# Cumulative sums of the gates as split single-pass products in a two-layer hybrid backbone

## The reference

```python
def gla_chunked(q, k, v, logg, s0, with_output=True):
    g = jnp.cumsum(logg.astype(f32).reshape(b, n, GLA_CHUNK, h, dk), axis=2)     # chunks of 64 positions
    g_last = g[:, :, -1]
    k_upd = k * jnp.exp(g_last[:, :, None] - g)
    ds = jnp.einsum('bnjhd,bnjhv->nbhdv', k_upd, v)
    decay = jnp.moveaxis(jnp.exp(g_last), 1, 0)
    ...                                           # scan of the states over the chunks
    g_mid = g[:, :, GLA_CHUNK // 2 - 1][:, :, None]
    scores = jnp.einsum('bnihd,bnjhd->bnhij', q * jnp.exp(g - g_mid), k * jnp.exp(g_mid - g))
    scores = jnp.where(mask, scores, 0.0)
    o_intra = jnp.einsum('bnhij,bnjhv->bnihv', scores, v)
    o_inter = jnp.einsum('bnihd,nbhdv->bnihv', q * jnp.exp(g), s_start)
    return (o_intra + o_inter).reshape(b, l, h, dv), s_final
...
logg_f = jax.nn.log_sigmoid((lr_f @ w_dec_f + b_dec_f).astype(jnp.float32)) / GLA_TAU
...
o = o_f + flip(o_b)                               # both directions, 4 heads, dk = 64, dv = 128
o = o * lax.rsqrt(jnp.mean(o * o, axis=-1, keepdims=True) + RMS_EPS)
y_gla = (o * gla_norm_w).reshape(b, l, GLA_V_W) * jax.nn.silu(r)
y = jnp.concatenate([y_gla, y_four, y_conv], axis=-1) @ w_out
```

## Time and profile before

| | us |
|---|---|
| median of three runs | 1609.99 |
| the profiled execution, its own time | 1608.07 |
| its span, first to last instruction | 1606.3 |
| TensorE busy in the span | 1542.8 (96%) |
| DVE, ScalarE, GpSimd busy | 861.7, 568.2, 592.9 |
| mean granted TensorE clock | 0.988 |

### The profile page before, as it was taken

The page is one execution under the profiler, slowest core; times in us unless marked ns, Lnnn a source line. Parts: engine busy times, 40 slices in busy tenths (PEclk is TensorE's granted clock), DMA queues, the critical chain, the costliest instruction groups (busy, mean ns, idle before and its releaser), DMA issues.

```text
span 1606.3 us, 22916 instructions
## 1 busy us (share of the span) xinstructions
PE 1542.8 (96%) x9056; PEld 1388.5 (86%) x9056; DVE 861.7 (54%) x1316; ACT 568.2 (35%) x916; POOL 592.9 (37%) x309
## 2 busy tenths in 40 slices
PE   5999999999999999999999989999999999999997
PEld 2899999886899999999998769888898888888887
DVE  1576888536756326661465675477656332322237
ACT  4644214425444214441243255432525321231221
POOL 0532211245325524653255223332152544444441
PEclk9999999999999999999999999999999999999999
DMA  9544431355322212222122341653040333322321
GB/s 370 199 166 153 160 123 62 113 172 206 118 63 70 79 37 95 74 72 66 53 80 91 119 158 53 209 198 105 28 158 27 107 106 128 128 94 92 104 82 63
DMA packets 54062, 183.93 MB, mean 115 GB/s; under 512 B 5650, under 2 KB 10642, under 8 KB 51028
## 3 DMA queue, kind: packets, MB, share of 16 engines
q1 hardware_dynamic: 47826, 168.85, 30.9%
q10 hardware_dynamic: 6146, 13.83, 2.5%
HBM read 171.13 MB, written 11.53 MB: 114 GB/s over the span
## 4 chain that ended last, share of the span: by engine, by line
PE 89%; DVE 3%; ACT 3%; DMA 2%; POOL 1%; issue 1%; SPq 1%; DVEq 0%; ACTq 0%; POOLq 0%
PE A L1022 61%; PE A L1274 8%; PE N L1274 4%; PE G L1274 4%; PE G L1329 1%; PE A L1208 1%; PE A L1202 1%; PE G L1177 1%; DMA raw<-modw 1%; PE G L1136 1%; DMA raw<-stream 1%; PE A L1170 1%; PE N L1190 1%; PE A L1216 1%; PE N L1120 1%
## 5 line engine op out<-in xcount | busy, mean ns | idle before, releaser
L960 POOL TENSOR_TENSOR w_lo<-raw,w_hi 128x1024 fp32r<-128x1024 f32 (+2 forms) x163 | 385.7, 2368 | 659.7 <-ACT w_hi L1356 622.5
L1022 PE MATMUL A<-h_hi,w_hi 128*128 128x512 f32 (+2 forms) x1264 | 416.3, 360 | 22.5 <-POOL h_lo L1005 10.4
L1022 PE MATMUL A<-h_hi,w_lo 128*128 128x512 f32 (+2 forms) x1264 | 406.2, 352 | 0.0
L1022 PE MATMUL A<-h_lo,w_hi 128*128 128x512 f32 (+2 forms) x1264 | 406.0, 352 | 0.0
L1356 ACT ACTIVATE w_hi<-raw 128x1024 fp32r<-128x1024 f32 (+2 forms) x163 | 167.3, 1028 | 379.2 <-PE A L1022 336.0
L1022 PEld LDWEIGHTS A<-h_hi,w_hi 128*128 128x128 f32 x1264 | 237.1, 192 | 66.1 <-POOL h_lo L1005 16.2
L1022 PEld LDWEIGHTS A<-h_hi,w_lo 128*128 128x128 f32 x1264 | 239.0, 192 | 22.0
L1022 PEld LDWEIGHTS A<-h_lo,w_hi 128*128 128x128 f32 x1264 | 239.4, 192 | 21.1 <-issue 0.5
L1022 PE MATMUL A<-g_hi,w_hi 128*128 128x384 f32 (+2 forms) x480 | 146.2, 347 | 3.8 <-DVE g_lo L1847 2.0
L1022 PE MATMUL A<-g_lo,w_hi 128*128 128x384 f32 (+2 forms) x480 | 145.2, 345 | 0.0
L1022 PE MATMUL A<-g_hi,w_lo 128*128 128x384 f32 (+2 forms) x480 | 145.0, 345 | 0.0
(11 more groups left out here) (313 smaller groups left out, 2648.2 us busy)
## 6 DMA issues: line engine op xcount, KB each, us to landing
raw<-stream SPq DMA_DIRECT2D x150, 512.0 KB, 3.7
mraw<-modv SPq DMA_DIRECT2D x54, 512.0 KB, 4.3
mraw<-modw SPq DMA_DIRECT2D x10, 1024.0 KB, 6.4
raw<-pairs SPq DMA_DIRECT2D x18, 512.0 KB, 4.8
raw<-modw SPq DMA_DIRECT2D x6, 1024.0 KB, 14.7
x<-x_keep ACTq DMA_DIRECT2D x4, 1536.0 KB, 13.5
raw<-stream SPq DMA_DIRECT2D x16, 384.0 KB, 3.1
bg<-modv SPq DMA_DIRECT2D x10, 512.0 KB, 4.1
```

Of the source, the lines that this page charges most:

```text
L960: pool.tensor_tensor(lo, like_chunk(n, raw[:, n % RAW, 0:WIDTH[n]]), hi.bitcast(F32), ALU.subtract).then_inc(lo_done, 1)
L1022: m = pe.matmul(dst[:, at:at + t1 - t0], a, b[:, k, t0:t1], start=(first and p == 0), stop=(last and p == 2))
```

## The change

Before a gate entry's products, the tile's logarithms (128x512, both directions) are split: ScalarE writes `ls_high`, rounded to fp32r, and GpSimd writes `ls_low`, the difference. The matrix, whose entries need no low part, is copied once to an fp32r view `mat_r`. Each float32 product is replaced by two single-pass ones, so a gate entry has four products of 128x256, eight for a tile. They wait for `lslo_ready`, which GpSimd raises.

The new work stands at these places. ScalarE: the matrix and the first tile's `ls_high` ahead of its first `four` share, every other tile's `ls_high` behind the exponentials of the tile before. GpSimd: `ls_low` at the tile's entry g = 0, behind whatever `low_until` emits there. That is the dft chunks for the first tile, and for tile number `at` of a layer the output projection's chunks below `at - 2`; before, these chunks came after the loop. The new buffers share space with others: `mat_r` with `mat`, `ls_low` with `wd`, `ls_high` with `mrow`.

```diff
@@ buffers and semaphores
+        ls_low_t, mat_t, ls_high_t = ExitStack(), ExitStack(), ExitStack()
+        with ls_low_t:
+            ls_low = sb("ls_low", [P, 512], F32R, stack=ls_low_t)
         wd = sb("wd", [97, 512])
         mask = sb("mask", [P, 2, P], I32)
+        with mat_t:
+            mat_r = sb("mat_r", [P, 4 * P], F32R, stack=mat_t)
         mat = sb("mat", [P, 4 * P + 2 * P + 2])
...
+        with ls_high_t:
+            ls_high = sb("ls_high", [P, 512], F32R, stack=ls_high_t)
         mrow = sb("mrow", [P, 512])
...
@@ GpSimd
+                if e[0] == "gate" and e[3] == 0:
+                    at = tiles_of(e[1]).index(e[2])
+                    low_until(PLAN.n0[e] + (max(0, at - 2) if at else RING))
+                    pool.wait_ge(lshi_ready, nth(e[1], e[2]) + 1)
+                    pool.tensor_tensor(ls_low[:, :], ls[:, e[2], :], ls_high[:, :].bitcast(F32),
+                                       ALU.subtract).then_inc(lslo_ready, 1)
                 if e[0] == "fold":
-                    low_until(PLAN.n0[("wout", e[1])])
+                    low_until(max(done[0], PLAN.n0[("wout", e[1])]))
@@ TensorE, entry gate
-                    read_out(pe, ("z", L, tt))
+                    pe.wait_ge(lslo_ready, nth(L, tt) + 1)
                     for pr in range(2):
-                        m = pe.matmul(G[g][:, pr * 256:(pr + 1) * 256], ls[:, tt, g * KW + pr * P:g * KW + (pr + 1) * P],
-                                      mat[:, g * 256:(g + 1) * 256], start=True, stop=True)
+                        own = slice(g * KW + pr * P, g * KW + (pr + 1) * P)
+                        pe.matmul(G[g][:, pr * 256:(pr + 1) * 256], ls_high[:, own], mat_r[:, g * 256:(g + 1) * 256],
+                                  start=True, stop=False)
+                        m = pe.matmul(G[g][:, pr * 256:(pr + 1) * 256], ls_low[:, own], mat_r[:, g * 256:(g + 1) * 256],
+                                      start=False, stop=True)
@@ ScalarE, entry four
+                    if nth(L, tt) == 0:
+                        act.wait_ge(consts_in, 16 * 4)
+                        link(act.activation(mat_r[:, :], mat[:, 0:4 * P], ACT.Copy))
+                    if tt == tiles_of(L)[0]:
+                        for t in tiles_of(L):
+                            read_out(act, ("z", L, t))
+                        act.activation(ls_high[:, :], ls[:, tt, :], ACT.Copy).then_inc(lshi_ready, 1)
@@ ScalarE, entry gate, after the exponentials
+                    at = tiles_of(L).index(tt) + 1
+                    if g and at < len(tiles_of(L)):
+                        act.activation(ls_high[:, :], ls[:, tiles_of(L)[at], :], ACT.Copy).then_inc(lshi_ready, 1)
```

More of the change, by code:

```diff
@@ L641, in bass_hybrid_block @@
         qk_ready, r_scaled = sem("qk_ready"), sem("r_scaled")
+        lshi_ready, lslo_ready = sem("lshi_ready"), sem("lslo_ready")
         osq_ready, orstd_ready, yg_ready, yhi_ready, ylo_ready = (
```

## The result

| | before | after |
|---|---|---|
| median of four runs, us | 1608.87 (1607.39 to 1610.87) | 1644.87 (1641.62 to 1648.07) |
| ratio, 95% interval | | 1.0225 [1.0207, 1.0243] |
| profiled execution, own time and span | 1608.07, 1606.3 | 1648.07, 1646.3 |
| mean granted TensorE clock | 0.988 | 0.976 |

The changed kernel is slower by 36.0 us by the medians; 33.4 was forecast from the profiled execution. The profiled execution of the changed kernel is the longest of its four, 40.0 above that of before.

What follows compares the result with a forecast made beforehand. TensorE, 89% of the chain, was taken to bound the kernel. Waits behind GpSimd's queue (20.8 us, product gains included) plus half clock (12.6) gave 33.4 over 1608.07: 1641.5, or 1643.4 by the median; forecast 1642.5, range 1629 to 1652.

Steps and rivals of the forecast that it cites:

- third gate, layer 0, with clock: Layer 0's third gate waits for the subtraction behind GpSimd's fold: `o` ends 4.3 us later, plus 2.1 for the clock.
- third gate, layer 1, with clock: The same wait behind fold in layer 1: 2.7 us after the shorter products, plus 2.1 for the clock.
- later rounds, with clock: Fourth and later gates wait behind an output-projection chunk: rounds 11.2 us instead of 7.79, four cost 13.8, clock extra.
- clock: TensorE at half clock behind each of six waits: 2.1 us each, 12.6 in all, bounds 10.2 and 18.6.
- The products: Eight single-pass gate products 0.12 us apart, 0.96 a tile instead of 1.92; ten tiles save 9.6 if nothing else moves.
- the upper bound: GpSimd's subtraction takes 1.95 us beside busy DVE; the lower bound, DVE quiet, is 1.29, and 1.3 was taken.
- the short end: Clock price per wait taken as 2.1 of 1.7 to 3.1 us, since `o`'s small products may not slow fully.
- The clock stayed high: Rival: no half clock behind the tile loops' waits, only the 20.8 us remain, 1629 to 1631; chance 0.13.
- The long end: Rival: clock low most of each round, subtraction 1.95, second path adds 0.5: 45 us, 1653; 0.11 together with dear products.
- Products that stay dear: Rival: two single-pass gate products still take 1.92 us, ten times 0.96 more, 1651; 0.11 together with the long end.
- GpSimd not late: Rival: low parts ready in time, each gate gives 0.96 back except where the mask limits; 6.7 us faster, 1602; chance 0.04.
- the second path in a round: Gate through exponentials, msq, DVE's products and rounding to the square: 5.5 us, up to 0.5 a round extra, taken as 0.

Runs made afterwards that it cites:

- e4: Changed kernel with 31 or 34 extra single-pass TensorE products filling each wait for the subtraction, from the third tile on; 1631.54 us.
- e10: e9 plus output-projection chunks' high parts made by ScalarE within msq, their low parts on GpSimd held until DVE finished the tile's output; 1606.19 us.
- e8: Changed kernel with its split, queue and waits, but the gates' products in float32 as before and no matrix copy; 1646.9 us.
- e1: Changed kernel with GpSimd's subtraction ahead of fold for the third tile and one output-projection chunk less ahead of it for later tiles; 1611.05 us.
- e9: Changed kernel with the low parts subtracted by DVE instead of GpSimd, whose queue is as before the change; 1608.03 us.
- e2: Changed kernel with only the third tile's subtraction moved ahead of fold, in both layers; 1635.18 us.
- e6: e1 with ScalarE's rounding for fourth and later tiles, and the output-projection chunks' high parts, moved into msq ahead of its waits; 1612.71 us.

## Why the prediction was right, point by point

It forecast 1642.5, and 1644.87 was measured. Its steps, with the rounds written as what they add to 7.79:

| step | forecast | measured |
|---|---|---|
| third gate, layer 0, with clock | +6.85 (4.3 + 0.45 + 2.1) | +7.56 |
| third gate, layer 1, with clock | +5.25 (2.7 + 0.45 + 2.1) | +5.51 |
| later rounds, with clock | +5.55 each | +6.22 +6.10 +5.98, and +5.83 |
| first tiles and first rounds | -0.9 in all | -0.6 |
| sum of the two loops | 33.4 | 36.6 |
| six waits, idle | near 26 | 27.3 |
| clock | 12.6 (10.2 to 18.6) | 13.3 (e4) |

*The products.* 0.12 us apart, as taken from the earlier trace rows. A gate saves less than the 0.96 that the prediction took, even at full clock and with nothing to wait for: 0.77 (e10), since the first product costs 0.22 and the old gate 1.83 by its starts, where the chain's row says 1.92. e8 shows that beneath the waits the ten gates bring 2.0 and not 9.6. The sum came out all the same, since what e8 gives back is in the clock's term, and that was read from the trace's own stretches.

*The queue.* Third gate forecast at 276.9, measured at 276.74. From the end of `o` to the fourth gate 5.35 were forecast, and 291.08 - 285.54 = 5.54 measured; the forecast had counted from the start of the square, which comes 0.21 later. GpSimd's subtraction took 1.26 against 1.3: DVE is idle there, so the lower bound held. That it can nearly double beside DVE was the upper bound's point, and e1 shows it. The prediction says that the trace has no such subtraction with 512 columns. It has 90, of weights (L1000): 27 and 18 of them with a median of 1.29 us and 45 with a median of 2.00. They give the same two bounds, so nothing hangs on it.

*The clock.* All six waits were followed by half clock. The Trainium skill (TensorE: Matmul & The Clock Gate, HAM oscillation) describes a loop that restarts cold on every pass; the windows at 0.50 and the 0.81 and 0.84 of the loops agree. Its price in the six rounds, after less e4, is 2.83, 2.35, 2.23, 2.10, 2.09 and 1.93, where 2.1 was taken. The reason given for taking the short end did not hold. The small products of `o`, for which no row existed, do slow down: 8 records of L1219 take 1.71 at 0.50 and 1.09 after it. What kept the price low is that each stretch of 6.8 us began in the wait, 0.7 to 2.4 us ahead of the gate, so that 6.1 to 4.5 us of it fell on work; the price is a little under half of that. That 2.1 came so near is in part luck. A later round at full clock (e4) is 3.87 over before and not 3.45: about 0.2 are the start of the square, 0.1 the gate, which takes 1.06 and not 0.96, and 0.15 the later start of e4's own gate. Of the 3.2 us missing from the sum, 1.7 are the four later rounds at full clock, 0.9 is the clock, 0.3 the third gate of layer 1 (3.42 at full clock, 3.15 forecast) and 0.3 the first rounds.

*Rivals.* The clock stayed high only where e4 filled the waits. The long end did not come: the subtraction ran beside an idle DVE, and half clock held for 4.5 to 6.1 us of work and not for the whole of each round. Products that stay dear are refuted by the distance of starts. GpSimd not late was rightly given little, but its price was wrong: the prediction set it at 1602 from TensorE's own work and from the path by way of the mask. e1 removed the lateness and measured 1611.05, and e9 took the subtraction off GpSimd as well, with 1608.03. The step that failed is the one by which each gate "would give its 0.96 back": the prediction had looked at the second path in a round (5.5 us from the gate's end to the square) and compared it with the short end of TensorE's work in a waiting round, but never closed it to a cycle, though the squares of the earlier trace rows stand 7.54 apart. With 7.54 as the floor the last two middle rounds of layer 0 give 0.24 each (e9); those of layer 1 give 0.77, which is all that a gate has to give, and not 0.96. The eight rounds of e9 save 2.6 us together, where 6.7 had been forecast with the first tiles.

*The rest of the program.* Forecast as unchanged within 2 us; the profiled execution moved there by 3.4 (3.1, 0.6 and -0.3). That is more than the prediction's own condition allowed. The bound was too narrow for single executions: in e2 and e4 the stretch between the loops, with the same program, took 830.1 and 826.2 us.

## What to carry to other kernels

Work that is put in an in-order queue inherits the lateness of everything ahead of it: a 1.26 us subtraction made TensorE wait 4.2 to 5.4 us in each of six rounds here, because it was placed behind work that had been harmless as long as nobody waited for it. Before counting what a cheaper step on the busiest engine gives, follow every cycle of the loop once round and read its period from two equal instructions of the other engines; the gain ends at the next longest. And price a new wait with what follows it: here the clock added 13.3 us to 27.3 us of waiting.

## What the runs showed of the hardware that was not expected

- GpSimd's subtractions and DVE's products, each with two SBUF inputs, did not run side by side although their records overlap (2.25 and 1.75 us against 1.26 and 0.68 apart). The later one ended a fixed time after the earlier one, 0.55 us for the product of 128x512, 1.08 for that of 128x1024 and 1.13 for GpSimd's subtraction (e1). What it costs is thus a wait for the other's end, and which one waits is set by the order of their starts. On DVE alone, between its own products (e9), the subtraction added nothing to the late rounds.
- DVE's operation of the same size with one operand from TensorE's result kept its 0.68 beside a busy GpSimd (e6).
- More work at once behind a wait didn't make the stretches of half clock longer: 6.8 us in all six with the cheap gates, 6.8 in three and 3.4 in three with the float32 gates of e8, which were up to 1.5 us longer each and cost 2.0 us in all. That the longer gates made them shorter isn't shown, since the clock also fell at another moment.
